# Gated linear attention between dense projection blocks: each unit's scores, outputs, gating and flips one or more blocks apart

## The reference, cut to what matters

```python
b = jnp.cumsum(log_a.reshape(shp_k), axis=2)      # cumulative log decay in a chunk
a_fwd = einsum(q * exp(b - mid), k * exp(mid - b)); a_rev = einsum(q * exp(mid - b), k * exp(b - mid))
o_intra = einsum(where(lower, a_fwd, a_rev), v)
u_c = einsum(k * exp(b_last - b), v)              # (dk, dv) of a chunk
state = dec * state + upd                         # scan over chunks
o_inter = einsum(q * exp(b), state_in)
o = o_intra + o_inter
o = o * rsqrt(mean(o * o) + EPS) * head_gain
o = o * silu(og)
```

## Time and profile before

| | us |
|---|---|
| median of 3 runs (2222.22 to 2347.48) | 2226.24 |
| the profiled execution's own time | 2223.73 |
| span of its slowest core (core 4) | 2221.9 |
| spans of all cores | 2207.3 to 2221.9 |
| PE busy, share of the span | 2034.3, 92% |
| DVE, ACT, POOL busy | 597.5, 493.2, 75.1 |

### The profile page before, as it was taken

How to read it: one execution, slowest core, us unless ns; L and a number is a source line. 1 busy time by engine, 2 the same in 40 slices (tenths; PEclk the granted TensorE clock), 3 DMA queues, 4 the chain that set the end, 5 groups by cost and what they waited for, 6 DMA issues and landing times.

```text
span 2221.9 us, 25571 instructions; the slowest of 8 cores (2207.3 to 2221.9 us)
## 1 busy us (share of the span) xinstructions
PE 2034.3 (92%) x9936; PEld 934.7 (42%) x9936; DVE 597.5 (27%) x908; ACT 493.2 (22%) x1045; POOL 75.1 (3%) x107
## 2 busy tenths in 40 slices
PE   2889889899999999999899999999999999996694
PEld 1344334444444444444344444444444444443342
DVE  3562554443322121124510101100110000015335
ACT  2463444420011111113500000000000000015444
POOL 0000000000000000000000000000000000000000
PEclk9998998999999999999999999999999999998897
DMA  7154040443444554375854443444444444355043
GB/s 201 57 131 79 8 70 1 72 71 64 79 77 68 84 81 67 63 152 149 216 95 76 81 75 70 93 76 76 76 76 78 78 83 83 77 132 142 1 86 152
DMA packets 49747, 194.20 MB, mean 87 GB/s; under 512 B 3259, under 2 KB 4667, under 8 KB 43612
## 3 DMA queue, kind: packets, MB, share of 16 engines
q0 software_dynamic: 38640, 137.44, 36.5%
q1 hardware_dynamic: 10988, 55.13, 7.4%
HBM read 313.20 MB, written 16.78 MB: 149 GB/s over the span
## 4 chain that ended last, share of the span: by engine, by line
PE 81%; DVE 6%; DMA 5%; ACT 4%; issue 3%; DVEq 0%; SPq 0%; ACTq 0%; POOL 0%; POOLq 0%
PE bank L367 79%; ACT arena L355 4%; DVE arena L358 3%; DVE arena L361 2%; DMA arena<-w_v 1%; PE bank L375 1%; DMA arena<-w_ffu 1%; DMA arena<-xp 1%; DMA arena<-gpost 1%; DMA arena<-w_mix 1%; DVE arena L507 1%; DVE arena L421 0%; DMA out<-arena 0%; DVEq L157 0%; SPq L388 0%
## 5 line engine op out<-in xcount | busy, mean ns | idle before, releaser
L367 PE MATMUL bank<-arena 128*128 128x512 bf16 (+4 forms) x9280 | 1990.7, 376 | 68.8 <-DVE arena L358 30.1
L367 PEld LDWEIGHTS bank<-arena 128*128 128x128 bf16 (+2 forms) x9280 | 891.9, 99 | 1144.9 <-issue 145.7
L358 DVE TENSOR_TENSOR arena<-bank,arena 128x512 f32<-128x512 f32 (+4 forms) x432 | 313.8, 738 | 1419.5 <-PE bank L367 1214.0
L355 ACT ACTIVATE arena<-bank 128x512 f32<-128x512 f32 (+7 forms) x400 | 223.5, 561 | 1472.0 <-PE bank L367 1066.3
L355 ACT ACTIVATE arena<-arena 128x1 f32<-128x1 f32 (+4 forms) x456 | 240.4, 541 | 180.6 <-DVE arena L361 98.7
L375 PE MATMUL bank<-arena 128*128 128x128 bf16 x656 | 54.8, 236 | 89.1 <-DVE arena L421 41.4
L375 PEld LDWEIGHTS bank<-arena 128*128 128x128 bf16 x656 | 44.5, 106 | 112.1 <-issue 108.2
L361 DVE SCALAR_TENSOR_TENSOR arena<-arena 128x512 f32<-128x512 f32 (+3 forms) x73 | 83.9, 1150 | 13.9 <-DMA out<-arena 6.8
L358 DVE TENSOR_TENSOR arena<-arena 128x512 f32<-128x512 f32 (+3 forms) x144 | 75.2, 527 | 16.1 <-ACT arena L355 5.3
L343 POOL DMA_DIRECT2D arena<-w_ffu x44 | 30.9, 702 | 619.4 <-PE bank L367 543.2
L361 DVE SCALAR_TENSOR_TENSOR arena<-bank,arena 128x256 f32<-128x256 f32 (+2 forms) x64 | 33.3, 521 | 45.0 <-PE bank L367 29.7
(11 more groups left out here) (25 smaller groups left out, 37.1 us busy)
## 6 DMA issues: line engine op xcount, KB each, us to landing
arena<-w_ffu POOLq DMA_DIRECT2D x44, 1024.0 KB, 8.4
arena<-w_gate POOLq DMA_DIRECT2D x16, 1536.0 KB, 13.8
arena<-w_fd POOLq DMA_DIRECT2D x16, 1408.0 KB, 9.6
arena<-x SPq DMA_DIRECT2D x16, 1024.0 KB, 6.9
arena<-w_conv POOLq DMA_DIRECT2D x8, 1536.0 KB, 14.0
arena<-xp SPq DMA_DIRECT2D x8, 1024.0 KB, 6.7
arena<-w_mix POOLq DMA_DIRECT2D x4, 2048.0 KB, 16.7
x1s<-arena SPq DMA_DIRECT2D x8, 1024.0 KB, 11.2
```

The costliest lines, as they stand in the source:

```text
L355: P.emit("act", lambda e: e.activation(out=out, in_=in_, func=func, **kw), reads=reads, writes=writes, partw=partw)
L358: P.emit("dve", lambda e: e.tensor_tensor(out=out, in0=in0, in1=in1, op=op), reads=reads, writes=writes, partw=partw)
L367: P.emit("pe", lambda e, l=l, r=r, j=j: e.matmul(out_ap, lhsT=l, rhs=r, start=(start and j == 0), stop=(stop and j == n - 1)), reads=reads ...
```

## The change

The attention's work is put into slots, one for each dense block. A table `then` maps a slot to what is emitted behind its dense block, `first_of` (filled by `ahead`) to what is emitted before it (`pre()`).

- The decay chain is cut into four parts: `one` (softplus), `two` (scan and subtractions), `three` (four Exps), `four` (the small copy), in slots one apart.
- A unit's `near` is in slot g, its `far` in g+2, the last product (`gated`) ahead of slot g+3, the flip in g+4. Units begin two slots after their step ends.
- The `og_block`s of a step move into the middle of the next step; those of the last step come right before the convolution, behind the load of the first convolution weights. So the first step has 8 blocks, the others 12. The og product on VectorE (`late`) is ahead of the next slot, and there GpSimd multiplies the gate by the head's gain (32 multiplies 128x256 fp32 in all), which takes the gain out of `far`; `on` goes, and `gated` is one product.
- The copies of the state to bf16 go from ScalarE to VectorE (64 of them), beside the update they precede.
- q times exp(b) is one product instead of two, and `far` writes the two chunks' halves of the output with two 64-column matmuls in place of two over all 128 rows. The six memsets go.
- Banks: `dense` has three instead of four, `little` five instead of four; `near` takes two (scores and the first update share one).
- The loads of w_v and w_og of the second pair are asked for at the ends of steps 1 and 2.

```diff
-    dense = Banks([0, 1, 2, 3])
-    little = Banks([4, 5, 6, 7])
+    dense = Banks([0, 1, 2])
+    little = Banks([3, 4, 5, 6, 7])
...
-            for par, o, n in ((0, qA, 4), (1, qB, 5)):
-                sel = lambda a, par=par: a.rearrange("p (i a t) -> p i a t", i=4, a=2)[:, :, par, :]
-                stt(sel(o), sel(bk[:, :]), QSCALE, sel(Eb), ALU.mult, ALU.mult, [bb, Eb_[0]], [bb_[n]])
+            stt(qe, bk[:, :], QSCALE, Eb, ALU.mult, ALU.mult, [bb, Eb_[0]], [bb_[4]])
...
-            tt(sg, bk[:, :], sg, ALU.mult, [bb, SOb[i]], [SOb[i]])
+            def late():
+                tt(sg, bk[:, :], sg, ALU.mult, [bb, SOb[i]], [SOb[i]])
+                for hh in range(2):
+                    o = sg[:, hh * 256:(hh + 1) * 256]
+                    P.emit("pool", lambda e, o=o: e.tensor_tensor(out=o, in0=o, in1=hgb, op=ALU.mult), reads=[cb], writes=[SOb[i]])
+            ahead(slot["n"] + 1, late)
...
-                act(sbf_r[n].ap, S[:, h, :], AF.Copy, [Sb[h]], [sbfb[n]])
+                P.emit("dve", lambda e, n=n: e.tensor_copy(out=sbf_r[n].ap, in_=S[:, h, :]), reads=[Sb[h]], writes=[sbfb[n]])
...
-            mm(bk[:, 0:256], bb, [(atT_r[i % 2].ap, v_r[self.j].ap[:, i, hh * 256:(hh + 1) * 256]),
-                                  (qA[:, ts], sbf_r[n0].ap), (qB[:, ts], sbf_r[n1].ap)],
-               [atTb[i % 2], vb[self.j][i], qkb[4], qkb[5], sbfb[n0], sbfb[n1]])
+            for hf, n in ((0, n0), (1, n1)):
+                t0 = i * 128 + hf * 64
+                mm(bk[hf * 64:(hf + 1) * 64, 0:256], bb, [(qe[:, t0:t0 + 64], sbf_r[n].ap)], [sbfb[n]], first=False, start=False)
...
-            stt(on_r.ap, bk[:, 0:256], hs[:, 2:3], hgb, ALU.mult, ALU.mult, [bb, hb_, cb], [onb])
-            tt(ubt_r[i].ap[:, hh * 256:(hh + 1) * 256], on_r.ap, SO_r[i].ap[:, hh * 256:(hh + 1) * 256], ALU.mult, [onb, SOb[i]], [ubtb[i]] if hh == 0 else (), [ubtb[i]] if hh else ())
+        def gated(self, hh, i):
+            stt(ubt_r[i].ap[:, cs], bk[:, 0:256], hs[:, 2:3], SO_r[i].ap[:, cs], ALU.mult, ALU.mult, [bb, hb_, SOb[i]], [ubtb[i]] if hh == 0 else (), [ubtb[i]] if hh else ())
...
-        seq = [lambda: stp.q_block(0), lambda: stp.k_block(0), lambda: (eprep_for(n, 1), stp.v_block(0)), lambda: (stp.k_flip(0), stp.v_block(1)),
-               lambda: stp.v_block(2), lambda: stp.q_block(1), lambda: stp.k_block(1)]
+        mid = [lambda i=i, p=steps[n - 1]: p.og_block(i) for i in range(4)] if n > 0 else [lambda: stp.v_block(0), lambda: stp.v_block(1)]
+        blocks = [lambda: stp.q_block(0), lambda: stp.k_block(0)] + mid + [lambda: stp.q_block(1), lambda: stp.k_block(1)]
+        blocks += [lambda i=i: stp.v_block(i) for i in range(0 if n > 0 else 2, 4)]
...
+        for g, f in ((g0 + 1, d1.one), (g0 + 2, d1.two), (g0 + 3, d1.three), (q1 - 1, d1.four), (g0 + 3, lambda p=stp: p.k_flip(0)), (q1 + 3, lambda p=stp: p.k_flip(1))):
+            after(g, f)
+        if n < 3:
+            d0 = decays[2 * n + 2]
+            for g, f in ((q1 + 1, d0.one), (q1 + 2, d0.two), (q1 + 3, d0.three), (nxt - 1, d0.four)):
+                after(g, f)
+        for u, (hh, i) in enumerate([(hh, i) for hh in range(2) for i in range(4)]):
+            g = nxt + 2 + u
+            ahead(g + 3, lambda p=stp, a=hh, i=i: p.gated(a, i))
+            if hh == 1:
+                after(g + 4, lambda p=stp, i=i: p.out_flip(i))
+            after(g + 2, lambda p=stp, a=hh, i=i: p.far(a, i))
+            after(g, lambda p=stp, a=hh, i=i: p.near(a, i))
```

More of the change, by code:

```diff
@@ L668, in __init__ @@
         def __init__(self, n):
-            self.pair, self.half = n // 2, n % 2
+            self.n, self.pair, self.half = n, n // 2, n % 2
             self.j = n % 2
@@ L694, in k_block @@
             s_ = self.sets[hh]
-            _, _, kf, kr, _, _ = [r.ap for r in QK_r[s_]]
+            _, _, kf, kr, _ = [r.ap for r in QK_r[s_]]
             bb_ = QKb[s_]
@@ L820, in build_program @@
[L820 to L834 removed]
+    then, first_of = {}, {}
@@ new lines, in build_program, with after, ahead, pre @@
+    slot = {"n": 0}
+    def after(n, f):
+        then.setdefault(n, []).append(f)
+    def ahead(n, f):
+        first_of.setdefault(n, []).append(f)
+    def pre():
+        for f in first_of.pop(slot["n"], ()):
+            f()
+    def run_small():
+        for f in then.pop(slot["n"], ()):
+            f()
+        slot["n"] += 1
+    steps = [Step(n) for n in range(4)]
+    decays = [Decay(n // 2, n % 2) for n in range(8)]
+    wv_of, wo_of = {}, {}
+    def load_v(pair):
+        flat, wb = wload(w_v[pair])
+        wv_of[pair] = (k3(flat, 16), wb)
@@ new lines, in load_o, with seed @@
+    def load_o(pair):
+        flat, wb = wload(w_og[pair])
+        wo_of[pair] = (k3(flat, 16), wb)
+    def seed(pair):
+        wv, wvb = wv_of[pair]
+        for h in (pair * 2, pair * 2 + 1):
+            bk, bb = dense.next()
+            c0 = (h % 2) * 256
+            mm(bk[:, 0:256], bb, [(GT[:, c, h * 128:(h + 1) * 128], wv[:, c, c0:c0 + 256]) for c in range(16)], [GTb, wvb])
+            act(S[:, h, :], bk[:, 0:256], AF.Copy, [bb], [Sb[h]])
+    load_v(0)
+    load_o(0)
+    for f in (decays[0].one, decays[0].two, decays[0].three, decays[0].four):
+        f()
@@ L837, in build_program @@
         if stp.half == 0:
-            for h in (stp.pair * 2, stp.pair * 2 + 1):
-                bk, bb = dense.next()
-                c0 = (h % 2) * 256
-                mm(bk[:, 0:256], bb, [(GT[:, c, h * 128:(h + 1) * 128], wv[:, c, c0:c0 + 256]) for c in range(16)], [GTb, wvb])
-                act(S[:, h, :], bk[:, 0:256], AF.Copy, [bb], [Sb[h]])
-        while pending:
-            run_small()
-        pending = stp.small()
+            seed(stp.pair)
+        if n == 1:
+            load_v(1)
+        if n == 2:
+            load_o(1)
+            steps[2].wo = steps[3].wo = wo_of[1]
+    conv_w = [wload(w_conv[0])]
+    for i in range(4):
+        pre()
+        steps[3].og_block(i)
+        run_small()
     M.drop(wk_r, wal_r, wq_r, GT_r, aug_r)
@@ L892, in build_program @@
             run_small()
-    while pending:
-        run_small()
-    M.drop(gla_r, S_r, *kd_r, *v_r, *SO_r, *[r for rs in QK_r for r in rs], *E_r, *kT_r, *sbf_r, *ubt_r, *atm_r, *atT_r, on_r, jk_r, *dec_r)
+    assert not then and not first_of, (then, first_of)
+    M.drop(gla_r, S_r, *kd_r, *v_r, *SO_r, *[r for rs in QK_r for r in rs], *E_r, *kT_r, *sbf_r, *ubt_r, *atm_r, *atT_r, jk_r, *dec_r)
     M.drop(*ux_r, *u_r, *y_r, hal_r)
```

139 lines of the change are left out of this document (64 added, 75 removed).

## The result

The changed kernel takes 2173.95 us (median of 4 runs, 2173.05 to 2174.32) against 2224.23 us of the kernel before (median of 4 runs, 2221.40 to 2347.48). The ratio is 0.9777, 95% interval 0.9758 to 0.9797: 2.2% faster, some 50 us, where 2180.5 us and 2.05% were forecast.

The account below looks back on a forecast made before the run. The prediction took PE's idle time (31.4 us) and half clock (21.2 us) in the attention as the bound: 2223.7 - 52.6 + 4.5 + 2.65 = 2178.25, plus 2.5 to the runs' median, called 2180.5 us; range 2169 to 2202.

Parts of the forecast that it names:

- What bounds the kernel: In the attention with units, PE loses 31.4 us idle and 21.2 us to half clock: at most 52.6 us to gain.
- rival 2: In the attention, short waits keep the clock falling: 2199 us; chance 0.24 together with rival 1 and mixtures.
- New waits, 4.5 us: PE waits for late VectorE behind scans (1.3 us, twice), at second-head q and k blocks, and in the convolution.
- One fall of the clock, 2.65 us: With waits of at most 1.3 us alone, the clock falls seldom; one half-clock stretch was counted.
- The distances: With far and flip in later slots, the 14.8 us ahead of flips go whole, as do waits ahead of far.
- PE's work, 0: PE's matmul time stays the same; far's two 64-column matmuls save 3.5 us at most, or lose it.
- VectorE level with PE, slack by banks: In slots with a near, VectorE has 32.3 us against PE's 34.9 a step; small banks are the slack.
- ScalarE, "nobody waits for the rest long": ScalarE loses 26.3 us of state copies; its remaining activations, 3.2 us at most, fit a slot of 4.1.
- GpSimd: Its gain multiply takes 0.74 us, two a slot are 1.5 of 4.1 us, costing nothing on PE's path.
- rival 1: In the 16 og slots, GpSimd's multiplies hold VectorE, which becomes the bound: 2199.5 us; chance 0.24 with rival 2 and mixtures.
- Loads and prologue: w_og and w_conv loads cost 0, up to 3 us if late; the prologue's three dense banks 0, between -2 and +2.

Follow-up runs that it names:

- a_lump: The changed kernel with each decay chain in one piece again, all four parts in one slot: 2188.9 us, ratio 0.9821.
- a_dvegain: The changed kernel with the 32 multiplies by the head's gain on VectorE instead of GpSimd: 2187.4 us, ratio 0.9828.
- a_scan_late: The changed kernel with the scan of the next step's first chain two slots later in steps 1 and 2: 2177.1 us, ratio 0.9774.
- a_close: The changed kernel with the old distances of near, far, gating and flip, and the new banks: 2175.7 us, ratio 0.9799.
- b_banks: The kernel before with only the change's banks (three dense, five small, scores and first update sharing one): 2217.5 us in one run, against 2225.8.
- b_banks_chain_copy: The kernel before with the change's banks, the decay chain in four parts and the 64 state copies on VectorE: 2195 us, ratio 0.9853.
- a_oldbanks: The changed kernel with four dense and four small banks and three for each near; some outputs changed, time a lower bound: 2192.5 us, ratio 0.9851.
- a_actcopy: The changed kernel with the 64 state copies on ScalarE again: 2199 us, middle of two runs, 0.988 of the kernel before.

## Why the prediction was right, and where it was not

- *What bounds the kernel: right.* The bound of 52.6 us (31.4 idle, 21.2 clock) was taken but for 3.2 us. The change has single waits up to 1.11 us and no fall of the clock, so rival 2 is out. But it does not take a cluster: in a_lump each of two single waits of 4.43 us has a fall, in a_dvegain two of three single waits of 1.81.
- *New waits, 4.5 us: right in place, high in size.* 3.2 us. The two at the scan were to be 1.3 us and are 1.11; a_scan_late takes them away. Those at q and k blocks are 0.46, 0.22 and 0.16, and the convolution has almost none.
- *One fall of the clock, 2.65 us: there was none.* With the 1.3 us above, that is 4 of the 6.5 us between 2180.5 and 2173.95; the rest is the difference between the runs' medians, within their scatter.
- *"The distances": this step failed.* The prediction had the flips wait for the product that they turn, and credited the gap between gating and flip with 14.8 us. For some 13 of them the flips waited for a bank, and a_close, with the old distances, is as fast as the change. The sum came out right because it priced the waits, nearly all of which went, and not the edit that took them: as far as the distances go, that was luck. With banks enough and VectorE late, the flips of b_banks and b_banks_chain_copy do wait for their gating (1.47 and 1.10 us); the changed kernel has neither wait at the old distances either, since its VectorE is not late.
- *PE's work, 0: low by some 3 us.* A far takes 0.43 us in place of 0.34 (see the last section), 3 us in 32. The balance does not show it, because of another term that it leaves out: the matmul ahead of a wait is counted busy for some 0.27 us, where it takes 0.11 if the next one follows at once, and there are 30 such waits fewer. (Both from each matmul's record, cores 4 and 1.)
- *VectorE level with PE, slack by banks: right, and more than it said.* 32 products of 0.43 us more on VectorE bring back 11 us (a_dvegain), and the old banks some 17 (a_oldbanks).
- *ScalarE, "nobody waits for the rest long": right only because the copies moved.* a_actcopy prices that at some 22 us; the prediction counted the move as 26.3 us off an engine that nobody waits for long, and gave it no part of the gain.
- *GpSimd: 0.726 us for 0.74, and no wait for it.* The rule named there (the Trainium skill, SBUF — State Buffer, "Who interferes with whom") is borne out: 12 of the 64 state copies overlap a GpSimd multiply in time and took 423 to 833 ns, the other 52 took 279 to 295 (worked out from each copy's record, core 1). Each of the 12 began while a multiply ran and ended 0.15 us behind that multiply's end, so it stood for the whole rest of it. That is 4.6 us of VectorE's time, and rival 1 would have had 23.7; it was the lesser price: the same multiplies on VectorE cost 11 us (a_dvegain).
- *Loads and prologue: right.* No wait for w_og or w_conv. The first q block starts 0.5 us later than in the profile of before, and the wait for w_v is 1.4 us longer (3.00 for 1.61), which is within the 3 us that the prediction allowed.

What stays open: how the last 17 us or so divide among the later start of the units, the moved og blocks, the single gating product and the three q products; and neither the new distances on the old order nor the old distances with the old banks in the changed order were tried.

## What to carry to other kernels

When a matmul waits for another engine's product, ask which one ended last and which bank it had: a wait at a flip can be a wait for the bank of something else, and then moving the flip away need not help. Where engines in order hand work to one another, price the edits together: three edits that gave 0, 0 and 8 us alone gave 33 together; with the banks alone, the wait at a flip only went from the mask to the gating behind it. Undoing parts of the finished version (22 us for the copies) told more than adding them to the old one (0 us).

## What the runs showed of the hardware

What PE did before the clock fell: single waits of up to 1.11 us had no fall behind them, of three single waits of 1.81 us (a_dvegain, core 3) two had one, each of two single waits of 4.43 us (a_lump) had one, and 31.4 us in clusters of waits of 0.2 to 2.5 us cost eight stretches.

A far's two 64-column matmuls on the two halves of one bank start at the same time in the records (252.70 us, both), but the next matmul starts 0.23 us later, so that side by side they take what two full ones take, 2 x 0.11. The full one ahead of them takes 0.20 us until they start, where in the kernel before each of a far's three took 0.11 to 0.12: the pair made the far longer, not shorter.

A VectorE copy of 128x256 fp32 to bf16 that meets a GpSimd multiply of 0.73 us ends 0.15 us behind the multiply, in all 12 cases. In a_dvegain, without the multiplies, one copy of the 64 still took 487 ns: the one that met GpSimd's issue of a weight load (399.04 us).
